# A fused two-block kernel: another order at the end of a triangular inverse, five fills a pair, and two other orders on VectorE

## The reference

```
g = -jnp.exp(a_log.astype(f32)) * jax.nn.softplus(a_lin.astype(f32) + dt_bias.astype(f32))
...
a_mat = jnp.where(strict, jnp.einsum('bhncd,bhnsd->bhncs', kb, k) * decay, 0.0)
l_mat = a_mat + eye
t_mat = lax.linalg.triangular_solve(l_mat, jnp.broadcast_to(eye, l_mat.shape), left_side=True,
                                    lower=True, unit_diagonal=True)
u = jnp.einsum('bhncs,bhnsd->bhncd', t_mat, v * beta[..., None])
w = jnp.einsum('bhncs,bhnsd->bhncd', t_mat, kb * jnp.exp(gc)[..., None])
...
def step(state, inp):
    qd, qkc, uc, wc, kd, gl = inp
    v_new = uc - jnp.einsum('bhcd,bhde->bhce', wc, state)
    o = jnp.einsum('bhcd,bhde->bhce', qd, state) + jnp.einsum('bhcs,bhse->bhce', qkc, v_new)
    state = state * gl[..., None, None] + jnp.einsum('bhcd,bhce->bhde', kd, v_new)
    return state, o
```

## Time and profile before

| | |
|---|---|
| median of 3 runs | 1049.33 us (1049.19 to 1049.4) |
| profiled execution, its own time | 1048.86 us |
| its span | 1047.0 us |
| mean granted TensorE clock | 0.993 of full |
| busy PE / DVE / ACT / POOL | 1014.1 / 648.9 / 428.6 / 211.6 us |

### The profile page before, as it was taken

How to read it: one execution, slowest core, us unless ns; L and a number is a source line. 1 busy time by engine, 2 the same in 40 slices (tenths; PEclk the granted TensorE clock), 3 DMA queues, 4 the chain that set the end, 5 groups by cost and what they waited for, 6 DMA issues and landing times. The chain is left out here.

```text
span 1047.0 us, 14640 instructions
## 1 busy us (share of the span) xinstructions
PE 1014.1 (97%) x5678; PEld 818.2 (78%) x5678; DVE 648.9 (62%) x1074; ACT 428.6 (41%) x866; POOL 211.6 (20%) x157
## 2 busy tenths in 40 slices
PE   9999999999999999999899999999999998989997
PEld 5888888888766687788778788878887777877786
DVE  4244656622237778766736766776597777966726
ACT  4223333332357844331533434366522458124432
POOL 0010000000001262103100001100105673034892
PEclk9999999999999999999999999999999999989999
DMA  9277643233413352241423447444242113221402
GB/s 317 81 246 254 215 131 118 81 121 101 141 44 110 97 182 81 64 157 62 154 99 121 146 137 259 156 148 162 80 173 90 63 61 102 82 99 63 181 1 81
DMA packets 60820, 132.38 MB, mean 126 GB/s; under 512 B 6096, under 2 KB 6480, under 8 KB 60624
## 3 DMA queue, kind: packets, MB, share of 16 engines
q1 hardware_dynamic: 58304, 118.67, 33.6%
q0 software_dynamic: 2304, 12.58, 3.4%
q10 hardware_dynamic: 144, 0.20, 0.1%
HBM read 117.22 MB, written 14.22 MB: 126 GB/s over the span
## 5 line engine op out<-in xcount | busy, mean ns | idle before, releaser
L290 DVE TENSOR_TENSOR w_lo<-raw,w_hi 128x2048 fp32r<-128x2048 f32 x57 | 134.3, 2355 | 214.2 <-ACT w_hi L286 198.2
L286 ACT ACTIVATE w_hi<-raw 128x2048 fp32r<-128x2048 f32 x51 | 97.4, 1912 | 200.3 <-PE projections_ps L126 156.9
L124 PE MATMUL projections_ps<-projections_x_hi,w_hi 128*128 128x512 f32 x208 | 81.1, 390 | 0.4 <-ACTq L646 0.4
L126 PE MATMUL projections_ps<-projections_x_hi,w_lo 128*128 128x512 f32 x208 | 80.9, 389 | 0.0
L125 PE MATMUL projections_ps<-projections_x_lo,w_hi 128*128 128x512 f32 x208 | 80.9, 389 | 0.0
L124 PE MATMUL projections_ps<-w_hi,projections_x_hi 128*128 128x512 f32 x192 | 74.9, 390 | 0.0
L126 PE MATMUL projections_ps<-w_hi,projections_x_lo 128*128 128x512 f32 x192 | 74.7, 389 | 0.0
L125 PE MATMUL projections_ps<-w_lo,projections_x_hi 128*128 128x512 f32 x192 | 74.7, 389 | 0.0
L247 DVE SCALAR_TENSOR_TENSOR resid<-resid,mixer_cw 128x512 f32<-128x512 f32 x96 | 65.0, 746 | 0.0
L747 POOL TENSOR_TENSOR tok<-tok,attention_recip 128x512 f32<-128x512 f32 x8 | 8.3, 1042 | 229.9 <-DVE attention_recip L835 229.9
L124 PE MATMUL projections_ps<-w_hi,output_m_hi 128*128 128x512 f32 x128 | 51.2, 400 | 3.4 <-DVE resid L1560 2.4
(11 more groups left out here) (367 smaller groups left out, 2463.0 us busy)
## 6 DMA issues: line engine op xcount, KB each, us to landing
raw<-in_w_in SPq DMA_DIRECT2D x26, 1024.0 KB, 5.0
raw<-in_gdn_w_in SPq DMA_DIRECT2D x24, 1024.0 KB, 5.0
tok<-in_ada_w POOLq DMA_DIRECT2D x16, 768.0 KB, 6.2
raw<-in_w_out SPq DMA_DIRECT2D x8, 1024.0 KB, 5.0
qkv_kept<-mixer_ring SPq DMA_DIRECT2D x8, 1024.0 KB, 4.2
mixer_st<-qkv_kept SPq DMA_DIRECT2D x32, 256.0 KB, 2.9
raw<-in_gdn_w_out SPq DMA_DIRECT2D x7, 1024.0 KB, 5.1
resid<-in_att_bias SPq DMA_DIRECT2D x16, 256.0 KB, 2.7
```

What stands on the lines that cost most here:

```text
L124: nc.tensor.matmul(out, w_hi, x_hi, start=first, stop=False, skip_group_check=True)
L126: return nc.tensor.matmul(out, w_lo, x_hi, start=False, stop=last, skip_group_check=True)
L286: self.nc.scalar.activation(self.hi[s][:], self.raw[s][:], ACT.Copy).then_inc(self.hi_ready, 1)
L290: engine.tensor_tensor(self.lo[s][:], self.raw[s][:], self.hi[s][:], ALU.subtract)\
```

## The change

Six edits:

1. `invert_32` ends with the transpose into `Tc`, the rows of pair 0 (`scale_rows(0, 1)`), and then the transpose into `Uc`. Pair 1's rows (`scale_rows(1, 2)`) are scaled in the prologue behind the copies of Z0 and T, pair 2's and 3's at n = 14 of pair 0.
2. Pair 0's Z products get the banks 6 and 7, in place of `psZ`, and don't wait for `vr_ok` any more; V0 is kept in a tile of its own. The copies of pair 0's values move behind `scale_rows(1, 2)`, ahead of the copies of Z1.
3. In the prologue TensorE has the triples behind V0, Z0 and T, and both groups of T together.
4. In the chunk loop the two groups of a kind stand together at one of five places; VectorE's copies have places of their own. `turn_v` of a pair also waits for the copies of the values of the pair before.
5. In the first scan `add_group(0)` comes ahead of `masked(1)`.
6. `StepSizes.finish` is cut in two; in the second mixer the series comes one block later, between the two rests of a weight tile (L290).

```diff
+            def z_bank(j, grp):
+                return psZ[:, grp, :] if j else ps[:, 6 + grp, :]
...
-        SLOTS = (1, 3, 4, 5, 7, 8, 9, 11, 12, 13)
+        PARTS = (("V", 0), ("Z", 0), ("T", 0), ("V", 1), ("Z", 1))
+        PRODUCTS_AT = {1: ("V", 0), 5: ("Z", 0), 9: ("T", 0), 13: ("V", 1), 15: ("Z", 1)}
+        COPIES_AT = {7: (("Z", 0, 0),), 8: (("Z", 0, 1),), 11: (("T", 0, 0),), 12: (("T", 0, 1),),
+                     15: (("Z", 1, 0), ("Z", 1, 1))}
...  # turn_v
                 if j:
                     pe.wait_ge(u_ok2, at(i, 4, j - 1, 4))
+                    pe.wait_ge(vr_ok, at(i, 2, j - 1, 2))
...  # double
-                        pe.wait_ge(tc_ok, 2 * i + (2 if j else 1))
+                        pe.wait_ge(tc_ok, 3 * i + min(j + 1, 3))
...
                         pe.wait_ge(uc_ok, i + 1)
-                        pe.wait_ge(vr_ok, at(i, 2, j, grp + 1))
+                        if j:
+                            pe.wait_ge(vr_ok, at(i, 2, j, grp + 1))
...  # TensorE's prologue
                 last_triple(0)
-                last_triple(1)
-                for kind, lv, grp in doubling_parts(0):
-                    double(i, 0, kind, lv, grp)
-                    if kind == "T" and grp == 0:
-                        last_triple(2)
-                last_triple(3)
+                for n, (kind, lv) in enumerate(PARTS):
+                    for grp in range(2):
+                        double(i, 0, kind, lv, grp)
+                    if n < 3:
+                        last_triple(n + 1)
...  # invert_32
-                nc.vector.transpose(Uc[:].rearrange("p m c -> p c m"), blocks).then_inc(uc_ok, 1)
                 own.did(nc.vector.transpose(Tc[:].rearrange("p m s -> p s m"), blocks.rearrange("p c s -> p s c")))
                 own.wait()
-                first, later = slice(0, 8), slice(8, 8 * HB)
-                nc.vector.tensor_tensor(Tc[:, first], Tc[:, first], by_row[:, first], ALU.mult).then_inc(tc_ok, 1)
-                nc.vector.tensor_tensor(Tc[:, later], Tc[:, later], by_row[:, later], ALU.mult).then_inc(tc_ok, 1)
+                scale_rows(0, 1)
+                nc.vector.transpose(Uc[:].rearrange("p m c -> p c m"), blocks).then_inc(uc_ok, 1)
...  # VectorE's prologue
-                for kind, lv, grp in doubling_parts(0):
-                    doubled(i, 0, kind, lv, grp)
+                for kind in ("Z", "T"):
+                    for grp in range(2):
+                        doubled(i, 0, kind, 0, grp)
+                scale_rows(1, 2)
+                for grp in range(2):
+                    values_out(i, 0, grp)
+                for grp in range(2):
+                    doubled(i, 0, "Z", 1, grp)
...  # VectorE's fills
+                            if n in (3, 4):
+                                values_out(i, j + 1, n - 3)
+                            for part in COPIES_AT.get(n, ()):
+                                doubled(i, j + 1, *part)
+                            if j == 0 and n == 14:
+                                scale_rows(2, HB)
...  # first scan, VectorE
             steps_of(1)
+            add_group(0)
             masked(1)
...  # step sizes, second mixer, VectorE
-                    for s in range(2):
-                        w.rest(nc.vector, dve, s, b + 1)
+                    w.rest(nc.vector, dve, 0, b + 1)
+                    if b == 2:
+                        soft_steps.finish(dve).then_inc(g_ok, 1)
+                    w.rest(nc.vector, dve, 1, b + 1)
```

More of the change, by code:

```diff
@@ L360, in exponentials, with begin @@
         self.nc.scalar.activation(self.a_exp[:], self.a_log_row, ACT.Exp).then_inc(self.exp_ok, 1)
-    def finish(self, dve):
+    def begin(self, dve):
         nc, own = self.nc, self.own
-        x, _, u, z, z2, q = (self.soft[:, n] for n in range(6))
+        _, _, u, z, z2, q = (self.soft[:, n] for n in range(6))
         dve.wait_ge(self.exp_ok, 2)
@@ L373, in finish @@
         own.did(nc.vector.tensor_tensor(z2, z, z, ALU.mult))
+    def finish(self, dve):
+        nc, own = self.nc, self.own
+        x, _, u, z, z2, q = (self.soft[:, n] for n in range(6))
         own.wait()
@@ L847, in finish @@
                     .then_inc(y_done, 1)
-            scan_own, scan_rest, low, dte_of, steps_of, masked, rest_of_scan = scan_vector(dve)
+            scan_own, scan_rest, low, dte_of, steps_of, masked, add_group, rest_of_scan = scan_vector(dve)
             dve.wait_ge(conv.conv_done, 2 + CT1)
@@ L1646, in rest_of_scan @@
                                                op0=ALU.add, op1=ALU.mult)
-            return own, rest, low, dte_of, steps_of, masked, rest_of_scan
+            return own, rest, low, dte_of, steps_of, masked, add_group, rest_of_scan
         return sync, tensor, scalar, gpsimd, vector
@@ L1864, in at @@
             return i * (HB * per_head) + (per_head * j + k)
+        def z_bank(j, grp):
+            return psZ[:, grp, :] if j else ps[:, 6 + grp, :]
         def values_of(i, j):
             return vr[j % 2] if j else vr_first
-        def doubling_parts(j):
-            parts = []
-            for lv in range(2):
-                for kind in ("V", "Z", "T"):
-                    if kind == "T" and lv == 1:
-                        continue
-                    parts += [(kind, lv, grp) for grp in range(2)]
-            return parts
         LOGS = TT * V_HEADS
@@ L2186, in double @@
                     m = 4 * grp + c
-                    out = bank[:, grp, c * P:(c + 1) * P]
+                    out = bank[:, c * P:(c + 1) * P]
                     if lv and kind == "V":
@@ L2199, in double @@
                         for even, odd in BLOCK_PAIRS:
[L2200 removed]
+                            mm = nc.tensor.matmul(out[even, odd], V0[odd, m, :], Uc[odd, 8 * j + m, :],
                                                   start=True, stop=True)
@@ L2398, in fill @@
                                 turn_v(i, j + 1)
-                            if n in SLOTS:
-                                double(i, j + 1, *part_at(j + 1, n))
+                            if n in PRODUCTS_AT:
+                                for grp in range(2):
+                                    double(i, j + 1, *PRODUCTS_AT[n], grp)
                         elif i == 0:
@@ L2549, in evacuate @@
                     act.wait_ge(v_made, at(i, 4, j, q))
-                    if lv:
-                        act.wait_ge(z_made, at(i, 4, j, q - 2))
+                    if lv and (j or i):
+                        act.wait_ge(z_made, at(i, 4, j - 1, 2 + grp + 1))
                     elif j or i:
-                        act.wait_ge(z_made, at(i, 4, j - 1, 2 + q))
+                        act.wait_ge(z_made, at(i, 4, j - 1, q))
                     if lv:
@@ L2656, in _ @@
                 act.wait_ge(scales_ok, i * 3 + 3)
-                for kind, lv, grp in doubling_parts(0):
-                    evacuate(i, 0, kind, lv, grp)
+                for lv in range(2):
+                    for grp in range(2):
+                        evacuate(i, 0, "V", lv, grp)
                 if i:
```

40 lines of the change are left out of this document (21 added, 19 removed).

## The result

The changed kernel takes 1051.22 us (median of 20 runs, 1049.45 to 1052.44), the kernel before 1049.35 (20 runs, 1048.49 to 1050.65); the ratio is 1.0017, with a 95% interval of 1.0011 to 1.0023. That is 1.9 us more. The forecast was 1048.8, in a range of 1044.3 to 1051.8. The time lies in the range, but on the other side of the kernel before, and above the 1047.5 to 1050.5 of the likeliest case.

The account below looks back on a forecast made before the run. TensorE, busy 1014.1 of 1047.0 us, was taken as the bound. Terms -1.2 - 1.07 - 5.3 + 2.5 + 2.6 = -2.5, or -0.5 with head group 0's clock fall, gave 1046.8 or 1048.8 us; range 1044.3 to 1051.8.

Parts of the forecast that it names:

- the likeliest case: Held scaling with the clock falling in head group 0: 1048.8 us, own range 1047.5 to 1050.5, chance 0.38.
- Scan and step sizes: First scan and step-size projection: TensorE's waits of 1.43 and 1.07 us go, for -1.2 and -1.07 us.
- End of the inverse, head group 1: Second prologue: Z0's 1.94 us wait goes and the clock holds; first W 5.05 us earlier, -5.3 us in all.
- the rival "slower": Clock falls in head group 1 as well, between T and `turn_v`; 3.7 us come back: 1052.2 us, chance 0.14.
- End of the inverse, head group 0: First prologue: `scale_rows(1, 2)` is held by GpSimd's L1853, so W starts later: +2.5 us.
- The fall of the clock there: Head group 0: TensorE's standstill of some 3 us drops the clock: +2.0 us, at a little over one half.
- Pairs: Chunk loop: five fills save 0.4 us a pair, but `turn_v` waits for Z1's copies at the boundary: +2.6 us in all.
- the -0.5 at the last pair: Last pair, within the pairs' +2.6: `we`, which had waited 0.61 us for clips, gains 0.5 us.
- the scaling was held: Against the rival that head group 0's scaling isn't held: -0.2 there, no clock fall, 1044.1 us, chance 0.13.
- the five fills are no gain: Against the rival that boundary copies are hidden and pairs give -1.5: 1044.7 or 1042.7 us, chance 0.09.

Follow-up runs that it names:

- scan_steps: Kernel before with only the two VectorE orders changed (add_group(0) ahead of masked(1); the series between the two rests): 1045.41 us, ratio 0.9974.
- busy: Changed kernel with 24 transposes that nothing reads in TensorE's 3.0 us standstill of the first prologue: 1048.07 us, ratio 0.9988.
- early_ten: scale_early with ten fills a pair in place of five, at the places of the kernel before: 1045.04 us, ratio 0.9953 to the kernel before.
- old_triples: scale_early with the triples of both prologues at their old places: 1049.05 us, ratio 0.9994 to the kernel before.
- mixed: scale_early with eight fills, V0, Z0 and T with both groups together, V1 and Z1 one by one: 1045.3 us, ratio 0.9961 to the kernel before.
- scale_early: Changed kernel with pair 1's rows scaled in invert_32, right behind those of pair 0: 1046.8 us, ratio 0.9985 to the kernel before.

## Why the prediction was wrong

But for the last pair of each head group, the mechanisms were as forecast; a sum of terms between -5.3 and +2.6 came out near zero, and three of them were off in the same direction: the price of the fall of the clock (+2.0, measured +3.1), the last pairs (-0.5, measured +0.6) and the second prologue (-5.05, measured -4.5).

**Scan and step sizes** (-2.27): right, -2.3 by three profiles and -2.7 by scan_steps (-1.5 to -4.0).

**End of the inverse, head group 1** (-5.3, with the half-clock work behind it): right in kind. The wait of 1.94 is gone and the clock holds; -4.5 for the prologue, where one profile of three has the clock low again at its end (3.4 us from 935.5, pair 0 at 17.11 in place of 16.14). That is the place that the rival "slower" had named. Against the one profile that the forecast was read from, with 15.86, the first of the changed kernel gives -5.2, as forecast; the two others of the kernel before are shorter.

**End of the inverse, head group 0** (+2.5): right to a tenth (2.44 by busy). A little of that is luck: the held scaling costs 2.17, not 2.7, and the prologue without it is 0.27 longer and not 0.2 shorter. The scaling took 3.39 us and ended 0.28 behind GpSimd's operation, as the port's rows had it. That agrees with the Trainium skill (SBUF — State Buffer, Who interferes with whom), in which a VectorE instruction with two SBUF inputs contends with a GpSimd instruction that reads SBUF, over ports that are an exclusive lock.

**The fall of the clock there** (+2.0): the case was the likeliest and came, but the price was 3.1 us. This is the first failed size. I took a value between 0.7 and 3.3, the prices of two lengths, 3.4 and 10 us. My 0.40 for each us of work at half clock was right (0.37 to 0.44), the amount of work was not: I had 5 us of it, and the three profiles have 6.8 to 8.6. The like place, the second prologue before, had 10.2 in all three profiles.

**Pairs** (+2.6): the boundary was right. The wait ahead of `turn_v` is 0.71 each time (forecast 0.6 to 0.7), the periods are 16.13 to 16.14 (16.15), and the pair with the clip costs 1.0 more (1.05). The ten fills of early_ten give the cost of the boundary directly: 0.52, and 0.89 with the clip. The step that failed is the -0.5 at the last pair, of which I wrote that `we` had waited 0.61 for clips. It now waits 0.96, and in head group 1 as well, where it had waited for nothing. I had weighed where the clip stands in VectorE's order and not who comes to the port first; Z1's copies between `es` and the clip hand it to GpSimd. -0.5 expected, +0.6 found: 1.1 us. It is the mechanism that I had used for the scaling.

**Sum**: fall +1.1, last pairs and tail +1.1, second prologue and its pairs +0.6, by the means of the profiles, and -0.2 from the other terms together. That is the way from -0.5 to +2.2.

Of the rivals, the scaling was held, the five fills are no gain (early_ten), and the clock held in the second prologue in two profiles of three. By the forecast's own bounds (slower above 1051.4) the time counts as the same, to which it gave 0.40; but it is slower clear of noise. The sum hardly had a sign to forecast: it set some 8 us of gain against 7.6 of cost, and a miss of 0.5 in either turned it.

## What to carry to other kernels

An operation that is moved on VectorE has to be read against GpSimd's timeline at its new place: with two inputs in SBUF it ends behind whatever GpSimd has begun, here 3 us for a scaling of 0.4. The same scaling one step earlier, where GpSimd stood still, took 0.4 us and held up nothing in head group 0.

A standstill of TensorE has two prices, the wait and the clock behind it. Where a low stretch has been seen, take its whole length, less what of it lies on the standstill, at the price that the rows give for work at half clock, here 0.4 us for each us. Profile a kernel more than once before a difference of 1 or 2 us is put down to a cause: the low stretches move by 3 to 7 us between executions of one program.

## What was not expected of the hardware

In all eighteen profiles each low stretch of the granted clock was 3.4, 6.8 or 10.2 us long, but for the one at the program's end. The clock also fell with no standstill above 0.84 us in the prologue (old_triples, 1.9 us behind it), and early_ten, mixed and scale_early, with the same second prologue, had it low for 6.8 us in one profile and not at all in three.
